# Attention's weights and values split into a rounded part and a remainder, multiplied in three passes

## The reference

```python
def latent_attention(q, k, v, kc, vc, sink):
    ...
        s_loc = jnp.einsum('bkgqd,bksd->bkgqs', qb, kb).astype(jnp.float32) * scale
        s_loc = jnp.where(valid, s_loc, NEG_INF)
        s_ctx = jnp.einsum('bkgqd,bksd->bkgqs', qb, kc).astype(jnp.float32) * scale
        p = softmax_with_sink(jnp.concatenate([s_loc, s_ctx], axis=-1), sink).astype(v.dtype)
        return (jnp.einsum('bkgqs,bksd->bkgqd', p[..., :span], vb)
                + jnp.einsum('bkgqs,bksd->bkgqd', p[..., span:], vc))
...
def merge(o_gla, gg, gla_norm, o_swa, w_o):
    B, H, T, DV = o_gla.shape
    og = rmsnorm(o_gla.transpose(0, 2, 1, 3), gla_norm).reshape(B, T, GLA_WIDTH) * jax.nn.silu(gg)
    osw = o_swa.transpose(0, 3, 1, 2, 4).reshape(B, T, SWA_WIDTH)
    return jnp.concatenate([og, osw], axis=-1) @ w_o
```

## Time and profile before

| | |
|---|---|
| median of 3 runs | 1780.54 us (1778.49 to 1783.59) |
| the profiled execution | 1780.42 us, span 1778.6 us |
| PE busy | 94% of the span |
| DVE, ACT, POOL busy | 59%, 38%, 55% |
| mean granted clock of PE | 0.983 |

### The profile page before, as it was taken

How to read it: one execution, slowest core, us unless ns; L and a number is a source line. 1 busy time by engine, 2 the same in 40 slices (tenths; PEclk the granted TensorE clock), 3 DMA queues, 4 the chain that set the end, 5 groups by cost and what they waited for, 6 DMA issues and landing times. The chain is left out here.

```text
span 1778.6 us, 27524 instructions
## 1 busy us (share of the span) xinstructions
PE 1677.5 (94%) x9466; PEld 1397.0 (79%) x9466; DVE 1054.2 (59%) x1629; ACT 677.3 (38%) x1186; POOL 977.5 (55%) x706
## 2 busy tenths in 40 slices
PE   4999999997999989989999999999989999999997
PEld 1899778896666654458888989998978889989986
DVE  2723564747576666625586665566685554555468
ACT  2413224304333434521244444444444444444441
POOL 1621545634161266700258777777797766776772
PEclk9999999997999999989999999999999999999999
DMA  8244565577353435513475313322325223313312
GB/s 314 83 113 165 191 217 177 190 205 219 100 157 112 130 119 150 156 62 120 141 218 185 87 56 94 94 63 78 95 71 176 82 75 94 94 47 94 94 50 104
DMA packets 211432, 225.64 MB, mean 127 GB/s; under 512 B 52752, under 2 KB 171664, under 8 KB 208144
## 3 DMA queue, kind: packets, MB, share of 16 engines
q1 hardware_dynamic: 209248, 224.46, 39.9%
q10 hardware_dynamic: 2096, 0.02, 0.1%
HBM read 177.22 MB, written 47.24 MB: 126 GB/s over the span
## 5 line engine op out<-in xcount | busy, mean ns | idle before, releaser
L2828 PE MATMUL ff_banks<-h_xop,h_whi 128*128 128x320 f32 x888 | 276.0, 311 | 12.3 <-DVE ff_part L2646 4.7
L2830 PE MATMUL ff_banks<-h_xop,h_whi 128*128 128x320 f32 x888 | 275.0, 310 | 0.0
L2829 PE MATMUL ff_banks<-h_xop,h_whi 128*128 128x320 f32 x888 | 275.0, 310 | 0.0
L2666 DVE TENSOR_TENSOR ff_acc<-ff_acc,ff_banks 128x512 f32<-128x512 f32 x294 | 199.1, 682 | 100.0 <-PE ff_banks L2857 99.9
L2855 PE MATMUL ff_banks<-h_wlo 128*128 128x512 f32 x600 | 233.9, 390 | 1.1 <-POOL h_whi L2526 1.1
L2857 PE MATMUL ff_banks<-h_wlo 128*128 128x512 f32 x600 | 233.4, 389 | 0.0
L2519 POOL TENSOR_TENSOR h_whi<-mid_raw,h_whi 128x512 fp32r<-128x512 f32 x154 | 214.7, 1410 | 6.1 <-ACT h_whi L2371 6.1
L2531 POOL TENSOR_TENSOR h_wlo<-mid_raw,h_wlo 128x320 fp32r<-128x320 f32 x128 | 116.9, 915 | 133.4 <-ACT mid_raw L2408 133.4
L2828 PEld LDWEIGHTS ff_banks<-h_xop,h_whi 128*128 128x128 f32 x888 | 167.3, 188 | 16.0 <-issue 8.7
L2829 PEld LDWEIGHTS ff_banks<-h_xop,h_whi 128*128 128x128 f32 x888 | 167.4, 189 | 1.1
L2830 PEld LDWEIGHTS ff_banks<-h_xop,h_whi 128*128 128x128 f32 x888 | 167.3, 188 | 0.0
(11 more groups left out here) (270 smaller groups left out, 3755.2 us busy)
## 6 DMA issues: line engine op xcount, KB each, us to landing
mid_raw<-in_w_ff SPq DMA_DIRECT2D x126, 512.0 KB, 4.4
mid_raw<-in_w_ada SPq DMA_DIRECT2D x18, 1024.0 KB, 7.2
early_room<-qk_by_channel SPq DMA_DIRECT2D x20, 512.0 KB, 4.3
proj<-prj_stage SPq DMA_DIRECT2D x60, 152.0 KB, 1.9
mid_raw<-in_w_in SPq DMA_DIRECT2D x6, 1216.0 KB, 6.4
early_room<-in_w_ada SPq DMA_DIRECT2D x6, 1024.0 KB, 11.1
decays<-early_room SPq DMA_DIRECT2D x8, 640.0 KB, 4.3
early_room<-decays SPq DMA_DIRECT2D x20, 256.0 KB, 2.9
```

The costliest lines, as they stand in the source:

```text
L2666: dve.tensor_tensor(acc[:, p, at], acc[:, p, at], down[n % RING], ALU.add).then_inc(added, 1)
L2828: pe.matmul(out, w_hi[:, k], x_hi[:, k], start=(k == 0), stop=False)
L2829: pe.matmul(out, w_hi[:, k], x_lo[:, k], start=False, stop=False)
L2830: mm = pe.matmul(out, w_lo[:, k], x_hi[:, k], start=False, stop=(k == KH - 1))
```

## The change

- The exponential is written to a ring of two (`prob`); ACT copies it rounded to fp32r (`phi`), POOL subtracts (`plo`). The values are split the same way once, `vhi` on ACT in beat 3 and `vlo` on POOL, from a raw copy that lies in the room of the output weights. The value product is three fp32r passes: vhi x phi, vlo x phi, vhi x plo.
- `kdup` is gone: raw scores of both heads take rows 0 to 63 of `khl` and `qdup`, and ACT makes one copy of each turned key group, not two.
- The gated output: POOL no longer squares, adds one, multiplies with the gate or scales with the gain. ACT squares, DVE makes the silu product in one instruction, the gain is folded into the first half of the output weights (`dve_gain`, 128x512, one slot ahead of the split), and `pool_scale` stands two slots behind `pool_sum`.
- The merge's first tile is rounded and split in halves, and its products begin on the first half; `pe_turn(1)` moves into the middle of `pe_products(0)`.

```diff
@@ class GlaOutput
-    def act(self, act, n):
+    def act_tanh(self, act, n):
...
+    def act_square(self, act, n):
+        act.wait_ge(self.o_ready, n + 1)
+        if n:
+            act.wait_ge(self.ssq_ready, n)
+        act.activation(self.sq[:, :], self.o[:, :], ACT.Square).then_inc(self.sq_ready, 1)
...
+    def dve_silu(self, dve, n):
+        j = n % 2
+        dve.wait_ge(self.tanh_ready, n + 1)
+        if n:
+            dve.wait_ge(self.out_ready, n)
+        dve.scalar_tensor_tensor(self.si[:, :], self.tanh[:, j], 1.0, self.gg[:, j], ALU.add, ALU.mult).then_inc(self.si_ready, 1)
@@ class OutputWeights
+    def dve_gain(self, dve, n):
...
+        rows = self.raw[:, n % 2, 0:GW // P]
+        dve.tensor_scalar(rows, rows, self.gain[:, 0:1], DH ** 0.5 / 2, ALU.mult, ALU.mult).then_inc(self.gained, 1)
@@ mixer, POOL
+                def low_weights(g):
+                    pool.wait_ge(phi_ready, g + 1)
+                    pool.tensor_tensor(plo[:, g % PRING], prob[:, g % 2], phi[:, g % PRING].bitcast(F32), ALU.subtract).then_inc(plo_ready, 1)
+
                 for w in range(SLOTS):
+                    low_weights(2 * w)
+                    low_weights(2 * w + 1)
                     if w in outputs_at and outputs_at[w] + 2 < X:
                         rec.pool_scaled(pool, outputs_at[w] + 2)
                     if w in glo_at:
                         glo.pool_sum(pool, glo_at[w])
-                    if w - 1 in glo_at:
-                        glo.pool_scale(pool, glo_at[w - 1])
+                    if w - 2 in glo_at:
+                        glo.pool_scale(pool, glo_at[w - 2])
@@ mixer, PE
-                    for e, rows in enumerate(sides):
-                        mm = pe.matmul(score[:, e, 0:PAST], qdup[rows, u % QRING, 2 * p + e], kdup[rows, kv, 0:PAST], start=True, stop=True)
+                    for e in range(2):
+                        mm = pe.matmul(score[:, e, 0:PAST], qdup[0:DH, u % QRING, 2 * p + e], khl[0:DH, kv, 0:PAST], start=True, stop=True)
...
-                    pe.wait_ge(p_ready, g + 1)
+                    pe.wait_ge(phi_ready, g + 1)
...
-                    pe.matmul(pv[0:DH + 1, :], vx[:, blocks(t)[b], kv], pT[:, g % PRING],
-                              start=(b == 0), stop=(b == count[u] - 1)).then_inc(pv_ready, 1)
+                    blk = blocks(t)[b]
+                    pe.matmul(pv[0:W, :], vhi[:, blk, kv], phi[:, g % PRING], start=(b == 0), stop=False)
+                    pe.matmul(pv[0:W, :], vlo[:, blk, kv], phi[:, g % PRING], start=False, stop=False)
+                    pe.wait_ge(plo_ready, g + 1)
+                    pe.matmul(pv[0:W, :], vhi[:, blk, kv], plo[:, g % PRING], start=False, stop=(b == count[u] - 1)).then_inc(pv_ready, 1)
@@ mixer, ACT
                 def weights(g):
                     act.wait_ge(st_ready, g + 1)
+                    if g >= 2:
+                        act.wait_ge(plo_ready, g - 1)
+                    act.activation(prob[:, g % 2], st[:, g % 2], ACT.Exp, scale=DH ** -0.5).then_inc(exp_ready, 1)
+
+                def high_weights(g):
+                    act.wait_ge(exp_ready, g + 1)
                     if g >= PRING:
                         act.wait_ge(pv_ready, g - PRING + 1)
-                    act.activation(pT[:, g % PRING], st[:, g % 2], ACT.Exp, scale=DH ** -0.5).then_inc(p_ready, 1)
+                    act.activation(phi[:, g % PRING], prob[:, g % 2], ACT.Copy).then_inc(phi_ready, 1)
@@ merge
+        if p == 0:
+            dve.wait_ge(self.mhi_half, 1)
+            dve.tensor_tensor(self.mlo[0][:, 0:KH], self.mT[:, 0:KH], hi_view(self.mhi[0])[:, 0:KH], ALU.subtract).then_inc(self.mlo_half, 1)
...
+            if p == 0 and half == 1:
+                self.pe_turn(pe, 1)
```

More of the change, by code:

```diff
@@ L1050, in __init__, with sp_gain @@
     def __init__(self, s, a, whi, wlo):
-        self.whi, self.wlo = whi, wlo
+        self.a, self.whi, self.wlo = a, whi, wlo
         self.raw = s.sb("wo_raw", [P, 2, KD, self.WC])
         self.w_in = [s.sem(f"wo_in{j}") for j in range(2)]
+        self.gain = s.sb("wo_gain", [P, 1])
+        self.gain_in, self.gained = s.sem("wo_gain_in"), s.sem("wo_gained")
         self.whi_ready, self.wlo_ready = s.sem("wo_hi_ready"), s.sem("wo_lo_ready")
         self.view = a["w_o"][0].rearrange("(k p) n -> p k n", p=P)
+    def sp_gain(self, sp):
+        for c in range(P // DH):
+            sp.dma_start(self.gain[c * DH:(c + 1) * DH, :], self.a["gla_norm"].rearrange("a d -> d a"), allow_slow_non_contiguous=True).then_inc(self.gain_in, 16)
     def columns(self, n):
@@ L1375, in mixer @@
         rec.rest(s)
-        kdup = s.sb("kdup", [P, KV, NB * P], F32R)
         khl = s.sb("khl", [P, KV, NB * P], F32R)
         kone = s.sb("kone", [EX, KV, NB * P], F32R)
-        vx = s.sb("vx", [P, NB, KV, DH + 1])
+        vhi, vlo = (s.sb(n, [P, NB, KV, W], F32R) for n in ("vhi", "vlo"))
         sink = s.sb("sink", [P, H])
@@ L1389, in mixer @@
         peak = s.sb("peak", [P, 2, EX], F32R)
-        pT = s.sb("pT", [P, PRING, HG * P])
+        prob = s.sb("prob", [P, 2, HG * P])
+        phi, plo = (s.sb(n, [P, PRING, HG * P], F32R) for n in ("phi", "plo"))
         oT = s.sb("oT", [DH + 1, HG * P])
-        junk = s.sb("junk", [P, 3 * P])
+        junk = s.sb("junk", [P, 3 * P], BF16)
         topc, topl, top, den, inv = (s.sb(n, [P, HG]) for n in ("topc", "topl", "top", "den", "inv"))
@@ L1572, in _ @@
                 pool.memset(maskr[:, 1, :], 0.0).then_inc(filled, 1)
-                pool.memset(vx[:, :, :, DH:DH + 1], 1.0).then_inc(filled, 1)
+                pool.memset(vhi[:, :, :, DH:W].bitcast(F32), 1.0).then_inc(filled, 1)
+                pool.memset(vlo[:, :, :, DH:W].bitcast(F32), 0.0).then_inc(filled, 1)
                 rec.pool_scaled(pool, 0)
@@ L1627, in raw_local @@
                     wait_room(("loc", u, p))
-                    for e, rows in enumerate(sides):
-                        mm = pe.matmul(score[:, e, 0:(hi - lo) * P], qdup[rows, u % QRING, 2 * p + e], kdup[rows, kv, lo * P:hi * P], start=True, stop=True)
+                    for e in range(2):
+                        mm = pe.matmul(score[:, e, 0:(hi - lo) * P], qdup[0:DH, u % QRING, 2 * p + e], khl[0:DH, kv, lo * P:hi * P], start=True, stop=True)
                     mm.then_inc(loc_ready, 1)
@@ L2073, in pe_products @@
             out = self.acc[:, j, half]
+            if p == 0 and half == 1:
+                self.pe_turn(pe, 1)
             for k in range(KD):
+                if p == 0 and half == 0 and k == KH:
+                    pe.wait_ge(self.mlo_ready, 1)
                 pe.matmul(out, self.mhi[j][:, k], self.whi[:, k, at], start=(k == 0), stop=False)
```

133 lines of the change are left out of this document (69 added, 64 removed).

## The result

The changed kernel takes 1848.41 us (median of 4 runs, 1846.29 to 1852.02). The kernel before, run beside it, took 1780.94 us (1778.49 to 1783.59). The ratio is 1.0381, with a 95% interval of 1.0359 to 1.0403: 68 us slower, where I had forecast 20 and had let the range end at 1828.

What follows compares the result with a forecast made beforehand. TensorE was taken as the bound in all three mixer windows, GpSimd second in the middle one. Terms +1.7 + 14 + 6 + 1 - 2.5 + 0 gave +20 us on 1780.42: 1800 us, range 1764 to 1828.

Steps and rivals of the forecast that it cites:

- The heavy rival: Mixer: VectorE chains caught repeatedly, TensorE idle over 2 us a pair and its clock dropping: 1830 us, chance 0.13.
- Raw scores (term 4): Raw scores of both heads in series cost 0.03 us for each of 72 pairs: +1, from 0 to +2.
- the rival I gave 0.05: Raw scores: row groups were running together, so 14 us more on TensorE: 1810 us, chance 0.05.
- A copy of this size is priced by the exponential: Each group's ScalarE copy takes 0.5 to 0.6 us, 64 us over the mixer.
- the loop: Mixer: subtraction, next slot's exponential, copy and two subtractions, through the ring of two, keep slots above about 3.85 us.
- Term 3: Slots 0 to 33: 17.5 us of stalls less 11.6 given back by TensorE: +6, from -12 to +30.
- TensorE gives back 34 x 0.34 = 11.6 us: Slots 0 to 33: three-pass value products save TensorE 0.34 us a slot; 20 us if it stays the bound everywhere.
- Term 1: Slots 49 to 57: 3.85 us a slot, 34.7 us against 33: +1.7, from -3 to +4.
- term 2: Slots 34 to 48: GpSimd's work and its conflicts with VectorE lengthen 62 us: +14, between +4 and +25.
- Term 5, the seam: Seam behind the mixer: products start 3.7 us earlier, turning of tile 1 moves behind: 2.5 us saved, 2 to 3.
- The rest: Single key copy, value split, lighter output stage, `junk` in bf16 and merged gain: 0, from -2 to +4.

Runs made afterwards that it cites:

- Experiment 5: The kernel before with one edit, both heads' raw scores on rows 0 to 63: 1796.74 us, ratio 1.0115.
- experiment 13: The base plus ScalarE copies, behind both exponentials, into a tile that nobody reads: 1810.81 us, ratio 1.0186.
- the kernel without the remainder: The changed kernel without GpSimd's subtraction, the third pass reading `phi`: 1807.51 us, ratio 1.0147.
- experiment 7: The changed kernel without remainder and copies, the exponential writing `phi` itself, still three passes: 1783.62 us, ratio 1.0030.
- experiment 8: The kernel without the remainder, its two copies moved behind the slot's query and output copies on ScalarE: 1787.99 us, ratio 1.0062.
- experiment 14: The base plus 116 GpSimd subtractions from a constant tile into one nobody reads or waits for: 1802.96 us, ratio 1.0151.
- the base: The kernel before with only the seam in halves and the lighter output stage of the change: 1782.51 us, ratio 1.0001.
- ring of four: The changed kernel, full computation, with four `prob` buffers and three each of `phi` and `plo`: 1844.92 us, ratio 1.0354.
- the early query copy: The kernel before with the seam in halves and ScalarE's query copy between the two exponentials: 1776.90 us, ratio 0.9971.
- experiment 2: The changed kernel with GpSimd subtracting constant tiles, nobody waiting, remainder left out of the result: 1838.36 us, ratio 1.0326.
- experiment 3: The changed kernel with an equally long GpSimd memset, which reads nothing, in place of the subtraction: 1816.24 us, ratio 1.0201.

## Why the prediction was wrong

The direction was right, the size not: +68 us where the sum had +20. The heavy rival (1830, chance 0.13) named the right mechanism for part of it. Two of the three large costs, the raw scores and the copies' place, stood in the sum at 1 and at nothing, so even the right direction rests on the third, the subtractions, alone. By steps of the prediction:

- **"Raw scores (term 4)": wrong, and shown.** I read a pair's 0.42 us as two passes in series at 0.225, and put +0.03 a pair, +1 in all. It was two passes side by side, started 3 ns apart, with a fixed part beside them: in series the pair of 512 takes 0.67, one pass of 0.25 more. Experiment 5 has the part alone at 20 us (15 to 26), where the rival I gave 0.05 said 14. What I compared was a pair's start-to-start time, which holds a fixed part beside the passes, with the spacing of a stream, which holds none. The start-to-start time of the single products just ahead, 0.42 and 0.32 us, shows it in the trace that I had.
- **"A copy of this size is priced by the exponential: ... 64 us over the mixer", and then nothing in the sum for what stands behind it on ScalarE: wrong, and shown.** The price was right (66 us) and its cover was not there. ScalarE was idle for most of the time, but two more instructions ahead of `qdup` and `oT` delay VectorE's `qlow` and through it TensorE: 33 us added alone (experiment 13), 21 taken out of the kernel without the remainder (experiment 7), 15 of them by place (experiment 8). This is the largest omission of the sum. I named only the loop, though my own account of the change has both copies ahead of all that follows.
- **Term 3: the stall right, the window wrong.** The window grew by 34 us, not 6. The stall that I priced at 17.5 us is about right: subtractions alone lengthen the window by 13 (experiment 14 against the base), and `early_mid` was at 728 ns (I had said above 0.8 us). What was missing is the rest: copies alone lengthen the same slots by 15.6, serial raw scores by 11.5, and the three passes give 4.5 where I had 11.6. TensorE's waits for `topc` and `qlow` grew. The small `peak`, at 780 ns against 309, was caught as well; I had not named it.
- **"TensorE gives back 34 x 0.34 = 11.6 us", 20 in all: the pace was right, the gain not.** Passes are 0.23 apart at full clock. Alone on the base the three passes were worth 4 us (-1 to 9): TensorE's work got shorter, and its waiting longer. That other engines' chains are nearly as long as its work fits this, and is argued, not shown.
- **Term 1 and term 2: undersized, and GpSimd wasn't what bounded them.** 44 us and 86.6 against my 34.7 and 76, and GpSimd was busy for 63 of 86.6 us, not over 85%. In slots 34 to 48 copies alone cost 11 us and subtractions alone 10. In slots 49 to 57 they cost 6 and 1, and the loop over the ring about 5 (44.2 us against 39.6 with a ring of four), while the ring of four shortens neither of the other windows by more than 0.2. Some 3 us of the last window come from parts together, and stay open.
- **Term 5, the seam: right.** 3.7 us (1.4 to 6.2) against 2.5. In the changed kernel the products start 2.58 us behind the turning.
- **The rest at 0: right within what was measured.** The lighter output stage costs 4 us (0 to 8). The single key copy and `vlo` weren't run alone.

Added each to a kernel that had none of the others, the parts make 20 (raw scores) + 33 (copies) + 27 (subtractions, unwaited) - 4 (three passes) - 4 (seam) + 4 (output stage) = 76 us, good to some 13; the change cost 68. With the 10 us of waits for `plo` it would be 86, so the prices overlap, and nothing large is left over. What share of the 20 us of the raw scores is still there in the full change is open: no kernel was run with the change and the raw scores on both halves. No kernel here beats the one before by more than the seam does (0.9979); the early query copy on top of it (0.9971) can't be told from it.

## What to carry to other kernels

Before pricing an instruction as hidden on an engine that is mostly idle, look at what stands behind it on that engine's list and who waits for that: two copies of 0.6 us a slot, on an engine 38% busy, cost 33 us, and moving them a few places down the list gave 15 of 21 back. A gain on a nearly full engine need not come through: of 20 us on paper 4 (-1 to 9) did here. And when two products on different halves of the partitions become two on one half, first compare the pair with one product alone, start to start.

## What the runs showed of the hardware

- Two raw-score products of 512 columns, each on 64 partitions, take 0.42 us from start to start of what follows when they lie on different halves, and 0.67 on the same half. The second starts 3 ns behind the first in the one case, 334 ns in the other. Serial order cost 20 us for 72 pairs, some of them of 384 columns or fewer.
- A GpSimd instruction that reads SBUF can hold up a VectorE instruction with two SBUF operands: one on 4 columns took 850 ns on average beside the subtractions (experiment 2) and 161 beside memsets of the same length (experiment 3), and VectorE's reductions of PSUM stay at 1223 ns beside both.
- TensorE's granted clock was part of most prices: in slots 34 to 48 it was 1.00 before and 0.75 after. Passes of 512 columns start 0.43 to 0.47 us apart where it was low and 0.23 where not (slots 52 and 53).
